# Weights split three blocks ahead of the products, with five blocks of high parts in place of four

## The chip, the cores and the metric

The kernel runs on one core of a Trainium2 chip. The metric is the device time of one execution in microseconds (us), the median of several. The engines are TensorE (PE; PEld is its weight load), VectorE (DVE), ScalarE (ACT), GpSimd (POOL) and SyncE (SP), which here only issues DMAs. Each runs its own list of instructions in order; they meet through semaphores.

## The reference

256 tokens behind 16 learned ones, width 1024, in fp32. First a hybrid block: one wide projection `w_in` feeds a gated delta rule (8 heads, chunks of 64), a sparse attention whose keys an indexer picks, and two gates; the two branches are mixed, and an MLP follows. Then a second block: a short convolution mixer, attention over a memory, a dense gated feed-forward, block attention, and a mixture of eight experts. The part around the change, in words of the reference:

```python
# delta branch
q, k, v = split(silu(causal_conv(cat(q, k, v), conv_w)))       # l2-normed, chunked delta rule
o = rmsnorm(o, norm_w) * silu(z)                                # "gated heads"
# sparse attention: score all keys with the indexer, keep the best, attend to them
s = einsum('bqhd,bsd->bqhs', qi, ki)
s = einsum('bqhs,bqh->bqs', relu(s), wi)
s = where(key_pos <= pos, s, -inf)
_, idx = lax.top_k(s, topk)                                     # topk = 64
p = softmax(where(valid, einsum(q, k_sel) * hd ** -0.5, -inf))
```

All matrix products with weights are meant at fp32 accuracy.

## The kernel before, in words

**Splitting.** TensorE multiplies in a rounded fp32 format (fp32r). For fp32 accuracy a factor is written as a high part (its rounding) and a low part (the rest), and a product is three matmuls, lines 433 to 435 in `mm3`: high by low, low by high, high by high.

**The stream of weights.** The weights are one long list `W` of blocks of up to 128 x 2048 numbers (1 MB), 143 before the experts and 33 for each expert. Four engines handle each block:
- SyncE loads it into a slot of the raw ring (line 396), 6 slots (8 in the experts), as soon as the block that held the slot is used;
- ScalarE casts it to its high part in a slot of the ring `hi_ring` (line 408). It waits for the block to land and, with NHI slots, for the products of block i - NHI;
- VectorE subtracts the high part from the raw block, in place (line 423), which leaves the low part;
- TensorE multiplies with both.

`act_high(q, upto)` casts all blocks up to number `upto` that aren't cast yet, at that place in ScalarE's list; `dve_low` does the same for VectorE. The calls are written into the code of each stage by hand, with the block whose products are next plus 2. Nothing else sets the order: each engine's list is fixed, and what it can't start yet holds what is behind it.

**Three low parts are GpSimd's.** `POOL_LOW` (line 411) names the blocks of aq 1 to aq 3, numbers 22 to 24; `dve_low` steps over them, and `pool_low` (line 429) makes them in stage index: two in a row, then the heads' gating (L1515, 8 instructions), then the third. av 0 is block 20, aq 0 block 21, gate_a 0 block 25.

**The stages** are load, delta, inverse, scan, index, dsa, mix, mlp, layer 0, dense, layer 1, experts. Two matter most here.

At the start TensorE multiplies the first blocks (the channels gk of the delta branch). ScalarE takes the results out of PSUM (L890, L897), VectorE runs the convolution's taps (L908), copies the 24 small columns out of PSUM (`dve_gate_small`, L766), and TensorE transposes these (L727).

In stage index TensorE multiplies the indexer's queries with its keys (L1608); ScalarE takes each head's scores through a relu out of PSUM (L1641), VectorE adds them up, weighed by head (L1682, `scalar_tensor_tensor` with two inputs in SBUF, 14 times). TensorE then sums the heads' squares (L1523) and goes on with the products of aq; ScalarE takes these out (L1632, `act_raw`). VectorE makes the norms (L1528, L1537) and then searches the best keys in `dve_best`: 8 rounds for each of two rows of queries, a MAX of eight (L1691) and a replacement (L1693), then the mask (L1697, L1699). Behind the search stand the gated heads (L1551), the ropes (L1575, L1581; L1565 on TensorE, L1570 on GpSimd), and the softmax rows of stage dsa.

Further places of the prediction: after `wo` (stage mix) the memory's keys and values (mk, mv) are multiplied, and VectorE copies them (L1982) ahead of the first blocks of the MLP.

Of the kernel before, what the change touches and what calls it, by code (L numbers as in the profile page):

```python
# [19 lines left out]
NRAW, NHI = 6, 4  # L20
# [243 lines left out]
def emit(A, cst, out, sem, counts, off, arena, arena_r, ring, ring_r, hi_ring, C, vec, sm, posi, ix, flag, bank):  # L264
# [799 lines left out]
    def act_delta_in(q):  # L1064
        for i in range(4):
            if i == 1:
                act_high(q, W.at["gk", 1] + 2)
                act_gate_rows(q)
            act_channels(q, "gk", i)
        act_silu(q, "gk", 7)  # L1070
        act_high(q, W.at["gq", 0] + 2)
# [24 lines left out]
        q.mark("delta_in")  # L1096

    def dve_delta_in(q):
        q.wait_ge(("in", "ident"))
        q.e.tensor_reduce(ident16, ident.rearrange("p (q c) -> p c q", c=16), AX, ALU.add).then_inc(*q.did(("ident16",)))  # L1100
        for i in range(4):
            if i == 1:
                dve_low(q, W.at["gk", 1] + 2)
# [173 lines left out]
    def act_base(q):  # L1277
        for r in range(4):
            act_high(q, W.at["gz", r] + 2)
            for j in (2 * r, 2 * r + 1):  # L1280
                q.wait_ge(("ps", "gz", j), ("ps", "vT", 16), ("ps", "l2", 15), ("metasq",), ("end", "delta_in", "pool"))
                q.e.activation(gz[:, j, :], B("gz", j)[:, 0:SEQ], ACT.Silu).then_inc(*q.did(("gz", j)))
                B.drop(("gz", j), ("gz", j))
                if j in (1, 4):
                    act_meta(q, {1: 2, 4: 4}[j])
                if j >= 6:
                    act_turn_blocks(q, groups[2 * j - 12])
                    act_turn_blocks(q, groups[2 * j - 11])
        act_meta(q, 8)

    def dve_base(q):
        dve_turn_blocks(q)
        for i in range(14, -1, -1):
            if i == 11:
                dve_meta_inverse(q, 1)
                dve_low(q, W.at["gz", 0] + 2)
            if i == 4:
                dve_low(q, W.at["gz", 1] + 2)
# [6 lines left out]
        dve_low(q, W.at["gz", 2] + 2)  # L1305
        dve_low(q, W.at["gz", 3] + 2)
# [142 lines left out]
    def act_scan(q):  # L1449
# [5 lines left out]
        for c in range(2):  # L1455
            for hp in range(0, 8, 4):
# [5 lines left out]
                act_high(q, W.at[name, r] + 2)  # L1462
# [7 lines left out]
    def dve_scan(q):  # L1470
# [4 lines left out]
        for c in range(2):  # L1475
            for hp in range(0, 8, 4):
                name, r, x0, n = BETWEEN[2 * c + hp // 4]
                dve_low(q, W.at[name, r] + 2)
# [165 lines left out]
    def act_index_in(q):  # L1644
        act_high(q, W.at["av", 0] + 2)
# [11 lines left out]
        for r in range(4):  # L1657
            act_high(q, W.at["aq", r] + 2)
# [42 lines left out]
    def dve_index_in(q):  # L1701
        dve_low(q, W.at["av", 0] + 2)
# [3 lines left out]
        dve_low(q, W.at["aq", 1] + 2)  # L1706
        dve_best(q)
        dve_low(q, W.at["aq", 2] + 2)
# [3 lines left out]
        dve_low(q, W.at["aq", 3] + 2)  # L1712
# [155 lines left out]
    def dve_branch_gates(q):  # L1868

        between = dve_ropes_between(q)  # L1870
        for name, dst in GATED:
            for r in range(4):
                for j in (2 * r, 2 * r + 1):
                    if j % 2:
                        dve_low(q, W.at[name, r] + 2)
# [6 lines left out]
    def act_branch_gates(q):  # L1882
        for name, dst in GATED:
            for r in range(4):
                act_high(q, W.at[name, r] + 2)
# [16 lines left out]
    def act_merge(q):  # L1902
        act_sigmoids(q)
        for r in range(4):
            act_high(q, W.at["wa", r] + 2)
        for r in range(4):
            act_high(q, W.at["wb", r] + 2)
# [6 lines left out]
    def dve_merge(q):  # L1914
        for r in range(4):
            dve_low(q, W.at["wa", r] + 2)
# [4 lines left out]
        for r in range(4):  # L1921
            dve_low(q, W.at["wb", r] + 2)
# [227 lines left out]
    def dve_mix(q):  # L2150
        for hf, k0, nk in row_blocks("wo", 8):
            dve_low(q, W.at["wo", hf, k0] + 2)
# [42 lines left out]
    def act_mlp(q):  # L2195
        for r in range(16):
            act_high(q, W.at["mlp_up", r] + 2)
# [11 lines left out]
        for hf, k0, nk in row_blocks("mlp_dn", 32):  # L2209
            act_high(q, W.at["mlp_dn", hf, k0] + 2)  # L2210
# [16 lines left out]
    def dve_mlp(q):  # L2227
        for r in range(16):
            dve_low(q, W.at["mlp_up", r] + 2)
# [6 lines left out]
        for hf, k0, nk in row_blocks("mlp_dn", 32):  # L2236
            dve_low(q, W.at["mlp_dn", hf, k0] + 2)
# [265 lines left out]
    def act_layer0(q):  # L2503
        for r in range(3):
            act_high(q, W.at["uc", r] + 2)
# [3 lines left out]
        for r in range(3):  # L2509
            act_high(q, W.at["uh", r] + 2)  # L2510
        act_high(q, W.at[("qm", 0), 0] + 2)
# [3 lines left out]
        for r in range(3):  # L2515
            act_high(q, W.at["ub", r] + 2)
# [3 lines left out]
        for hf, k0, nk in row_blocks(("o", 0), 8):  # L2520
            act_high(q, W.at[("o", 0), hf, k0] + 2)
# [4 lines left out]
    def dve_layer0(q):  # L2526
        for r in range(3):
            dve_low(q, W.at["uc", r] + 2)
# [3 lines left out]
        for r in range(3):  # L2532
            dve_low(q, W.at["uh", r] + 2)
# [9 lines left out]
        dve_low(q, W.at[("qm", 0), 0] + 2)  # L2543
        pairs = dve_pairs(q, mem0)
        for r in range(3):
            dve_low(q, W.at["ub", r] + 2)
# [8 lines left out]
        for hf, k0, nk in row_blocks(("o", 0), 8):  # L2555
            dve_low(q, W.at[("o", 0), hf, k0] + 2)
# [19 lines left out]
    def act_dense(q):  # L2576
        for j in range(11):
            act_high(q, W.at["dg", j] + 2)
# [8 lines left out]
            act_high(q, W.at["du", j] + 2)  # L2587
            for f in (2 * j, 2 * j + 1):
                act_split(q, gg.hi[:, f, :], gtmp[f % 4], ("gu", f), ("gghi", f))
        for hf, k0, nk in row_blocks("dd", 22):  # L2590
            act_high(q, W.at["dd", hf, k0] + 2)
# [4 lines left out]
    def dve_dense(q):  # L2596
        rest = dve_both_weighed(q, "a0")
        for j in range(11):
            dve_low(q, W.at["dg", j] + 2)
            dve_low(q, W.at["du", j] + 2)  # L2600
# [9 lines left out]
        for hf, k0, nk in row_blocks("dd", 22):  # L2610
            dve_low(q, W.at["dd", hf, k0] + 2)
# [40 lines left out]
    def act_layer1(q):  # L2652
        for r in range(3):
            act_high(q, W.at["kx", r] + 2)
# [3 lines left out]
        for r in range(3):  # L2658
            act_high(q, W.at["vx", r] + 2)
        for r in range(3):  # L2660
            act_high(q, W.at["qx", r] + 2)
# [4 lines left out]
        act_high(q, W.at[("qm", 1), 0] + 2)  # L2666
# [3 lines left out]
        for hf, k0, nk in row_blocks(("o", 1), 8):  # L2670
            act_high(q, W.at[("o", 1), hf, k0] + 2)
# [15 lines left out]
    def dve_layer1(q):  # L2687
        rest = dve_both_weighed(q, "b0")
        for r in range(3):
            dve_low(q, W.at["kx", r] + 2)  # L2690
# [5 lines left out]
        for r in range(3):  # L2696
            dve_low(q, W.at["vx", r] + 2)
# [5 lines left out]
        for r in range(3):  # L2703
            dve_low(q, W.at["qx", r] + 2)
# [4 lines left out]
        dve_low(q, W.at[("qm", 1), 0] + 2)  # L2709
# [4 lines left out]
        for hf, k0, nk in row_blocks(("o", 1), 8):  # L2714
            dve_low(q, W.at[("o", 1), hf, k0] + 2)
# [199 lines left out]
    def act_up(q, R, x):  # L2915
        for j, (c0, n, nk) in enumerate(UPS):
            act_high(q, R.w.at["up", x, j, 0, 8 - nk] + 2, R.w)
# [5 lines left out]
            act_high(q, R.w.at["up", x, j, 1, 8 - nk] + 2, R.w)  # L2923
# [378 lines left out]
```

## Time and profile before

| | |
|---|---|
| median of 3 runs | 1872.31 us (1871.34 to 1874.65) |
| the profiled execution | 1868.43 us, span 1866.6 us |
| mean granted clock of TensorE | 0.985 |
| TensorE busy | 1810.5 us, 97% |
| VectorE busy | 1393.0 us, 75% |
| ScalarE busy | 1073.5 us, 58% |
| GpSimd busy | 119.8 us, 6% |
| moved by DMA | 438.91 MB, mean 235 GB/s |

The span runs from the first to the last instruction of the profiled execution; busy times are shares of it. In rows of a timeline the first number is the start in us from the span's start, the second how long the group of `xN` like instructions took, and the bracket holds the idle time of the engine before it and what ended that. An arrow reads "written from". A clock of 1.00 is 2.4 GHz, 0.50 is 1.2 GHz.

### The profile page before, as it was taken

To read this page: it belongs to the slowest core of one execution; us is meant where nothing else is said; L and a number is where in the kernel's file an instruction comes from. 1 tells how busy PE (TensorE), PEld (TensorE's weight loads), DVE (VectorE), ACT (ScalarE), POOL (GpSimd) and SP (SyncE) were. 2 spreads that over 40 slices of the span, in tenths; PEclk is the share of its full clock that TensorE was granted. 3 is DMA by queue.
4 is the path that set the end of the run, shared out by engine and by line. 5 is a ranking of instruction groups with operands and counts; after the bars stand their busy time and mean duration, and the time that the engine had idled before them with its cause. 6 is when DMAs were issued, how large, how long until landed. Compare 5 with 4: busy or idle time off the path is not lost.

```text
span 1866.6 us, 26784 instructions
## 1 busy us (share of the span) xinstructions
PE 1810.5 (97%) x11434; PEld 1626.3 (87%) x11434; DVE 1393.0 (75%) x1621; ACT 1073.5 (58%) x1188; POOL 119.8 (6%) x123
## 2 busy tenths in 40 slices
PE   9999999999999999999998899999999999999997
PEld 8999988999998898998896788888888888888885
DVE  6796387566665466655675789898989898889887
ACT  7653344545554444543344477777767677777674
POOL 2353152000000000000010000000000000000000
PEclk9999989999999999999998799999999999999999
DMA  8332224455655454665553289989998999899993
GB/s 285 107 103 69 91 91 136 154 197 178 195 180 190 162 178 150 201 203 169 170 181 113 90 309 370 374 312 377 351 379 309 377 352 379 322 364 368 359 371 138
DMA packets 258983, 438.91 MB, mean 235 GB/s; under 512 B 10309, under 2 KB 131736, under 8 KB 258728
## 3 DMA queue, kind: packets, MB, share of 16 engines
q1 hardware_dynamic: 258856, 437.11, 67.1%
q8 instruction: 92, 1.51, 0.3%
q14 instruction: 35, 0.29, 0.0%
HBM read 436.04 MB, written 1.05 MB: 234 GB/s over the span
## 4 chain that ended last, share of the span: by engine, by line
PE 85%; DVE 5%; ACT 2%; issue 1%; POOL 0%; DVEq 0%; ACTq 0%; POOLq 0%
PE bank L435 25%; PE bank L433 25%; PE bank L434 25%; PE bank L2886 1%; PE bank L2833 1%; PE bank L1785 1%; DVE ring_r L423 1%; PE bank L2396 1%; PE bank L1331 1%; PE bank L1323 1%; ACT arena L2418 1%; DVE arena L1693 0%; DVE arena L1581 0%; PE bank L1336 0%; PE bank L2984 0%
## 5 line engine op out<-in xcount | busy, mean ns | idle before, releaser
L423 DVE TENSOR_TENSOR ring_r<-ring,hi_ring 128x2048 fp32r<-128x2048 f32 x403 | 910.3, 2286 | 261.8 <-ACT hi_ring L408 261.6
L408 ACT CAST hi_ring<-ring 128x2048 fp32r<-128x2048 f32 x406 | 761.4, 1904 | 151.7 <-PE bank L435 147.4
L433 PE MATMUL bank<-hi_ring,arena_r 128*128 128x512 f32 (+1 forms) x1542 | 573.9, 372 | 0.0
L434 PE MATMUL bank<-ring_r,arena_r 128*128 128x512 f32 (+2 forms) x1550 | 572.9, 370 | 0.0
L435 PE MATMUL bank<-hi_ring,arena_r 128*128 128x512 f32 (+1 forms) x1542 | 572.1, 371 | 0.0
L433 PE MATMUL bank<-ring_r,hi_ring 128*128 128x256 f32 (+1 forms) x1400 | 400.6, 286 | 6.0 <-DVE ring_r L423 2.7
L434 PE MATMUL bank<-ring_r,hi_ring 128*128 128x256 f32 (+1 forms) x1400 | 395.7, 283 | 0.0
L435 PE MATMUL bank<-ring_r 128*128 128x256 f32 (+1 forms) x1400 | 395.7, 283 | 0.0
L434 PEld LDWEIGHTS bank<-ring_r,arena_r 128*128 128x128 f32 (+1 forms) x1550 | 291.7, 188 | 51.6
L435 PEld LDWEIGHTS bank<-hi_ring,arena_r 128*128 128x128 f32 x1542 | 290.6, 188 | 50.5
L433 PEld LDWEIGHTS bank<-hi_ring,arena_r 128*128 128x128 f32 x1542 | 290.7, 188 | 50.2
L433 PEld LDWEIGHTS bank<-ring_r,hi_ring 128*128 128x128 f32 x1400 | 264.8, 189 | 8.6 <-DVE ring_r L492 3.1
L435 PEld LDWEIGHTS bank<-ring_r 128*128 128x128 f32 x1400 | 265.1, 189 | 0.0
L434 PEld LDWEIGHTS bank<-ring_r,hi_ring 128*128 128x128 f32 x1400 | 264.0, 189 | 0.2
L496 ACT CAST arena_r<-bank 128x512 fp32r<-128x512 f32 (+1 forms) x62 | 32.3, 526 | 73.3 <-PE bank L2886 66.6
L496 ACT CAST arena_r<-arena 128x256 fp32r<-128x256 f32 (+2 forms) x74 | 31.7, 432 | 72.5 <-DVE arena L2603 37.6
L2921 ACT ACTIVATE arena<-bank 128x512 f32<-128x512 f32 (+1 forms) x48 | 27.1, 564 | 68.2 <-PE bank L435 68.1
L492 DVE TENSOR_TENSOR arena_r<-bank,arena_r 128x512 fp32r<-128x512 f32 (+1 forms) x62 | 37.4, 607 | 12.5 <-ACT arena_r L496 12.5
L433 PE MATMUL bank<-arena_r,hi_ring 128*128 128x256 f32 x160 | 45.4, 284 | 0.0
L435 PE MATMUL bank<-arena_r,ring_r 128*128 128x256 f32 x160 | 45.3, 283 | 0.0
L434 PE MATMUL bank<-arena_r,hi_ring 128*128 128x256 f32 x160 | 44.9, 281 | 0.0
L1632 ACT ACTIVATE arena<-bank 128x256 f32<-128x256 f32 (+1 forms) x27 | 10.4, 385 | 57.0 <-PE bank L435 57.0
(397 smaller groups left out, 1621.9 us busy)
## 6 DMA issues: line engine op xcount, KB each, us to landing
ring<-in_w_gu_moe SPq DMA_DIRECT2D x176, 1024.0 KB, 6.2
ring<-in_w_down_moe SPq DMA_DIRECT2D x88, 1024.0 KB, 5.5
ring<-in_w_in SPq DMA_DIRECT2D x31, 1024.0 KB, 5.4
ring<-in_w_gu_dense SPq DMA_DIRECT2D x22, 1024.0 KB, 5.2
ring<-in_w_up SPq DMA_DIRECT2D x16, 1024.0 KB, 5.4
ring<-in_w_down SPq DMA_DIRECT2D x16, 1024.0 KB, 5.0
ring<-in_w_in_a SPq DMA_DIRECT2D x10, 1024.0 KB, 5.6
ring<-in_w_down_dense SPq DMA_DIRECT2D x10, 1024.0 KB, 5.1
```

The costliest lines, as they stand in the source:

```text
L408: q.e.copy(hi_ring[:, b:b + m], ring[:, a:a + m]).then_inc(*q.did(("hi", of.tag, i)))
L423: q.e.tensor_tensor(ring_r[:, a:a + m], ring[:, a:a + m], hi_ring[:, b:b + m].bitcast(F32), ALU.subtract).then_inc(*q.did(("lo", of.tag, i)))
L433: q.e.matmul(ps, a[0], b[0], start=first, stop=False)
L434: q.e.matmul(ps, a[0], b[1], start=False, stop=False)
L435: return q.e.matmul(ps, a[1], b[0], start=False, stop=last)
L492: q.e.tensor_tensor(lo, src, hi.bitcast(F32), ALU.subtract).then_inc(*q.did(*done))
L496: q.e.copy(hi, src).then_inc(*q.did(*done))
L1323: t = q.e.matmul(ps[:, x * P:(x + 1) * P], MTs[i % 3][:, x, :], D[:, m, :], start=True, stop=True)
L1331: t = q.e.matmul(ps[:, x * P:(x + 1) * P], Ys[i % 3][:, x, :], DT[:, m, :], start=True, stop=True)
L1785: t = q.e.matmul(ps[p0:p0 + hd, qt * P:(qt + 1) * P], u["v"](j)[0:n, :], pt[0:n, j, :], start=(x == 0), stop=(x == len(use) - 1))
L2396: t = q.e.matmul(ps[:, 65 * e:65 * e + 65], pt[:, x * P:(x + 1) * P], u["v"](j, 2 * e + par), start=(j == 0), stop=(j == nj - 1))
L2921: q.e.activation(hh[:, c0:c0 + n], R.banks(R.tag, "up", x, j, 0)[:, 0:n], ACT.Silu).then_inc(*q.did(("hsilu", R.tag, x, j)))
```

## The change

A constant AHEAD = 3 takes the place of the 2 at every call of `act_high` and `dve_low`; the ring of high parts gets a fifth slot (8 KB for each partition). The scratch memory that is set aside for dynamic DMAs is set to 4096 bytes when the program is built. The diff in its core (the same replacement stands at all other calls):

```diff
-NRAW, NHI = 6, 4
+NRAW, NHI, AHEAD = 6, 5, 3
...
     def act_channels(q, name, i):
         dst, w0, c0 = chan[name]
-        act_high(q, W.at[name, i] + 2)
+        act_high(q, W.at[name, i] + AHEAD)
...
     def dve_channels(q, name, i):
         dst, w0, c0 = chan[name]
-        dve_low(q, W.at[name, i] + 2)
+        dve_low(q, W.at[name, i] + AHEAD)
...
     def act_index_in(q):
-        act_high(q, W.at["av", 0] + 2)
+        act_high(q, W.at["av", 0] + AHEAD)
...
         for r in range(4):
-            act_high(q, W.at["aq", r] + 2)
+            act_high(q, W.at["aq", r] + AHEAD)
...
     def dve_index_in(q):
-        dve_low(q, W.at["av", 0] + 2)
+        dve_low(q, W.at["av", 0] + AHEAD)
...
-        dve_low(q, W.at["aq", 1] + 2)
+        dve_low(q, W.at["aq", 1] + AHEAD)
         dve_best(q)
-        dve_low(q, W.at["aq", 2] + 2)
+        dve_low(q, W.at["aq", 2] + AHEAD)
...
     def act_mix(q):
         for hf, k0, nk in row_blocks("wo", 8):
-            act_high(q, W.at["wo", hf, k0] + 2)
+            act_high(q, W.at["wo", hf, k0] + AHEAD)
...
     def dve_up(q, R, x):
         for j, (c0, n, nk) in enumerate(UPS):
-            dve_low(q, R.w.at["up", x, j, 0, 8 - nk] + 2, R.w)
-            dve_low(q, R.w.at["up", x, j, 1, 8 - nk] + 2, R.w)
+            dve_low(q, R.w.at["up", x, j, 0, 8 - nk] + AHEAD, R.w)
+            dve_low(q, R.w.at["up", x, j, 1, 8 - nk] + AHEAD, R.w)
...
-    nc = bacc.Bacc("TRN2", target_bir_lowering=False, num_devices=1)
+    nc = bacc.Bacc("TRN2", target_bir_lowering=False, num_devices=1, dynamic_dma_scratch_size=4096)
```

TensorE's list stays as it is. On VectorE, at the start of the program, before the first taps (L908); `ring_r` is the raw ring seen as fp32r, `hi_ring` the ring of high parts:

```order
 L423 TENSOR_TENSOR ring_r_49<-ring,hi_ring 128x2048
 L1100 TENSOR_REDUCE sm<-consts 128x16
-L423 TENSOR_TENSOR ring_r_49<-ring,hi_ring 128x2048
+L423 TENSOR_TENSOR ring_r_49<-ring,hi_ring 128x2048 x2
 L908 SCALAR_TENSOR_TENSOR arena<-bank2,vec,arena 128x271
 L908 SCALAR_TENSOR_TENSOR arena<-bank2,vec,arena 128x270
```

One subtraction more, that of block 3, stands ahead of the taps; ScalarE casts three blocks instead of two at that place.

On VectorE in stage index, between the norms of the heads and the search of the best keys:

```order
 L1684 TENSOR_TENSOR arena<-arena,consts 128x128
 L1537 RECIPROCAL sm<-sm 128x16
+L423 TENSOR_TENSOR ring_r_49<-ring,hi_ring 128x2048
 L1691 MAX arena<-arena 128x8
 L1693 MATCH_REPLACE arena<-arena 128x272
```

Before, nothing stood there, since block 24 is GpSimd's; now block 25 does.

On GpSimd in stage index, with the semaphores that each instruction waits for (act_index counts ScalarE's instructions of this stage):

```order
 L1510 TENSOR_TENSOR arena<-arena 128x256 x3
-L429 TENSOR_TENSOR ring_r<-ring,hi_ring 128x2048 [waits act_index] x2
-L1515 TENSOR_TENSOR arena<-arena 128x256 [waits act_inverse]
+L429 TENSOR_TENSOR ring_r<-ring,hi_ring 128x2048
+L429 TENSOR_TENSOR ring_r<-ring,hi_ring 128x2048 [waits act_index]
+L1515 TENSOR_TENSOR arena<-arena 128x256 [waits act_inverse,act_index]
 L1515 TENSOR_TENSOR arena<-arena 128x256 [waits act_inverse,pool_index]
```

The instructions are the same; what moved is what they wait for. The high part of block 22 is now cast in the stage before, and that of block 23 by the first instruction of ScalarE in this one.

## Rows read from the trace of the kernel before

**Rows 1.** Section 1 of the page: busy us, share of the span, instructions by engine

```profile
PE 1810.5 (97%) x11434; PEld 1626.3 (87%) x11434; DVE 1393.0 (75%) x1621; ACT 1073.5 (58%) x1188; POOL 119.8 (6%) x123
```

**Rows 2.** TensorE's waits: us in total, times, longest

```profile
PE bank L875 <- DVE sm L817: 2.9, 1, 2.9
PE bank L433 <- DVE ring_r L423: 2.7, 1, 2.7
...
PE bank L1608 <- ACT arena L1641: 2.2, 1, 2.2
...
PE bank L1785 <- ACT arena L1814: 2.0, 1, 2.0
```

**Rows 3.** Busy time by stretch: PE, PEld, DVE, ACT, POOL; then PEclk, DMA share, GB/s

```profile
200.00:250.00 50.00, 47.85 (x356) 45.18 (x355) 25.19 (x36) 20.15 (x39) 12.55 (x12) 0.92 0.32 99
250.00:300.00 50.00, 48.05 (x384) 46.57 (x381) 47.32 (x104) 23.25 (x40) 30.14 (x22) 0.98 0.41 127
300.00:448.00 148.00, 148.00 (x1126) 139.12 (x1124) 94.97 (x165) 77.12 (x138) 0.16 (x2) 1.00 0.51 168
1084.00:1866.00 782.00, 769.58 (x3701) 642.83 (x3699) 684.19 (x456) 554.02 (x409) 0.00 (x0) 1.00 0.95 345
```

**Rows 4.** Section 5 of the page, VectorE's subtraction for low parts

```profile
L423 DVE TENSOR_TENSOR ring_r<-ring,hi_ring 128x2048 fp32r<-128x2048 f32 x403 | 910.3, 2286 | 261.8 <-ACT hi_ring L408 261.6
```

**Rows 5.** Timeline of VectorE, 446 to 456 us: start, us, what, count, idle before

```profile
448.27 0.42 DVE L1982 COPY consts<-bank 128x256 f32<-128x256 f32 x1 [2.39 <-PE bank L435]
448.62 6.69 DVE L423 TENSOR_TENSOR ring_r<-ring,hi_ring 128x2048 fp32r<-128x2048 f32 x3
```

**Rows 6.** Section 3 of the page: queue, packets, MB, share

```profile
q1 hardware_dynamic: 258856, 437.11, 67.1%
```

**Rows 7.** Timeline of SyncE's queue, 0 to 30 us

```profile
13.26 5.30 SPq L396 DMA_DIRECT2D ring<-in_w_in  x3
```

**Rows 8.** Instructions of line 396 from 0 to 30 us, their landing

```profile
DMA to landing us min/median/max: 8.8/9.9/13.7
```

**Rows 9.** Timeline of VectorE, 23 to 28 us

```profile
23.68 3.04 DVE L908 SCALAR_TENSOR_TENSOR arena<-bank,vec,arena 128x271 f32<-128x271 f32 x6
...
26.69 0.40 DVE L766 COPY arena<-bank 24x272 f32<-24x272 f32 x1
```

**Rows 10.** Timeline of TensorE, 26 to 29 us

```profile
27.15 0.33 PE L727 MATMUL bank<-consts,arena 24*128 24x24 f32 x3
```

**Rows 11.** Timeline of ScalarE, 225 to 262 us

```profile
229.00 1.92 ACT L408 CAST hi_ring<-ring 128x2048 fp32r<-128x2048 f32 x1
...
240.23 0.29 ACT L1641 ACTIVATE arena<-bank 128x144 f32<-128x144 f32 x1 [0.18 <-DVE arena L1682]
...
257.25 1.90 ACT L408 CAST hi_ring<-ring 128x2048 fp32r<-128x2048 f32 x1
```

**Rows 12.** Timeline of VectorE, 230 to 300 us

```profile
252.93 0.38 DVE L1691 MAX8 arena<-arena 128x8 f32<-128x272 f32 x1
...
254.66 0.43 DVE L1691 MAX8 arena<-arena 128x8 f32<-128x272 f32 x1
...
272.45 2.71 DVE L1551 SCALAR_TENSOR_TENSOR arena<-arena,vec,bank 128x512 f32<-128x512 f32 x4
```

**Rows 13.** Instructions of line 1697: duration ns min/median/max

```profile
L1697 DVE TENSOR_SCALAR arena<-arena x2: 296/1320/2345, 267.1 to 269.7; 128x272 f32<-128x272 f32 x2
```

**Rows 14.** Timeline of GpSimd, 225 to 270 us

```profile
234.97 4.53 POOL L429 TENSOR_TENSOR ring_r<-ring,hi_ring 128x2048 fp32r<-128x2048 f32 x1
254.61 4.63 POOL L429 TENSOR_TENSOR ring_r<-ring,hi_ring 128x2048 fp32r<-128x2048 f32 x1 [15.11 <-ACT hi_ring L408]
...
264.78 4.53 POOL L429 TENSOR_TENSOR ring_r<-ring,hi_ring 128x2048 fp32r<-128x2048 f32 x1
```

**Rows 15.** Instructions of line 1682: duration ns min/median/max

```profile
L1682 DVE SCALAR_TENSOR_TENSOR arena<-arena,sm x14: 368/500/4456, 235.2 to 251.9; 128x144 f32<-128x144 f32 x7, 128x272 f32<-128x272 f32 x7
```

**Rows 16.** Timeline of TensorE, 236 to 246 us

```profile
240.75 5.47 PE L1523 MATMUL bank<-consts,arena 128*128 128x1 f32 x28
```

More of the change, by code:

```diff
@@ L1066, in act_delta_in @@
             if i == 1:
-                act_high(q, W.at["gk", 1] + 2)
+                act_high(q, W.at["gk", 1] + AHEAD)
                 act_gate_rows(q)
@@ L1070, in act_delta_in @@
         act_silu(q, "gk", 7)
-        act_high(q, W.at["gq", 0] + 2)
+        act_high(q, W.at["gq", 0] + AHEAD)
         act_gate_sums(q)
@@ L1102, in dve_delta_in @@
             if i == 1:
-                dve_low(q, W.at["gk", 1] + 2)
+                dve_low(q, W.at["gk", 1] + AHEAD)
                 dve_gate_rows(q)
@@ L1278, in act_base @@
         for r in range(4):
-            act_high(q, W.at["gz", r] + 2)
+            act_high(q, W.at["gz", r] + AHEAD)
             for j in (2 * r, 2 * r + 1):
@@ L1295, in dve_base @@
                 dve_meta_inverse(q, 1)
-                dve_low(q, W.at["gz", 0] + 2)
+                dve_low(q, W.at["gz", 0] + AHEAD)
             if i == 4:
-                dve_low(q, W.at["gz", 1] + 2)
+                dve_low(q, W.at["gz", 1] + AHEAD)
                 dve_meta_inverse(q, 2)
@@ L1304, in dve_base @@
         dve_meta_inverse(q, 4)
-        dve_low(q, W.at["gz", 2] + 2)
-        dve_low(q, W.at["gz", 3] + 2)
+        dve_low(q, W.at["gz", 2] + AHEAD)
+        dve_low(q, W.at["gz", 3] + AHEAD)
     steps = [(b, g) for b in (16, 32, 64) for g in groups[:4]]
@@ L1884, in act_branch_gates @@
             for r in range(4):
-                act_high(q, W.at[name, r] + 2)
+                act_high(q, W.at[name, r] + AHEAD)
                 yield
@@ L1904, in act_merge @@
         for r in range(4):
-            act_high(q, W.at["wa", r] + 2)
+            act_high(q, W.at["wa", r] + AHEAD)
         for r in range(4):
-            act_high(q, W.at["wb", r] + 2)
+            act_high(q, W.at["wb", r] + AHEAD)
             for j in (2 * r, 2 * r + 1):
@@ L1915, in dve_merge @@
         for r in range(4):
-            dve_low(q, W.at["wa", r] + 2)
+            dve_low(q, W.at["wa", r] + AHEAD)
             for j in (2 * r, 2 * r + 1):
@@ L1921, in dve_merge @@
         for r in range(4):
-            dve_low(q, W.at["wb", r] + 2)
+            dve_low(q, W.at["wb", r] + AHEAD)
             for j in (2 * r, 2 * r + 1):
@@ L2196, in act_mlp @@
         for r in range(16):
-            act_high(q, W.at["mlp_up", r] + 2)
+            act_high(q, W.at["mlp_up", r] + AHEAD)
             if r == 0:
@@ L2228, in dve_mlp @@
         for r in range(16):
-            dve_low(q, W.at["mlp_up", r] + 2)
+            dve_low(q, W.at["mlp_up", r] + AHEAD)
             for j in (2 * r, 2 * r + 1):
@@ L2504, in act_layer0 @@
         for r in range(3):
-            act_high(q, W.at["uc", r] + 2)
+            act_high(q, W.at["uc", r] + AHEAD)
             if r == 0:
@@ L2509, in act_layer0 @@
         for r in range(3):
-            act_high(q, W.at["uh", r] + 2)
-        act_high(q, W.at[("qm", 0), 0] + 2)
+            act_high(q, W.at["uh", r] + AHEAD)
+        act_high(q, W.at[("qm", 0), 0] + AHEAD)
         for j in range(2):
@@ L2515, in act_layer0 @@
         for r in range(3):
-            act_high(q, W.at["ub", r] + 2)
+            act_high(q, W.at["ub", r] + AHEAD)
             for j in (2 * r, 2 * r + 1):
@@ L2527, in dve_layer0 @@
         for r in range(3):
-            dve_low(q, W.at["uc", r] + 2)
+            dve_low(q, W.at["uc", r] + AHEAD)
             if r == 0:
@@ L2532, in dve_layer0 @@
         for r in range(3):
-            dve_low(q, W.at["uh", r] + 2)
+            dve_low(q, W.at["uh", r] + AHEAD)
             for j in (2 * r, 2 * r + 1):
@@ L2577, in act_dense @@
         for j in range(11):
-            act_high(q, W.at["dg", j] + 2)
+            act_high(q, W.at["dg", j] + AHEAD)
             if j == 0:
@@ L2598, in dve_dense @@
         for j in range(11):
-            dve_low(q, W.at["dg", j] + 2)
-            dve_low(q, W.at["du", j] + 2)
+            dve_low(q, W.at["dg", j] + AHEAD)
+            dve_low(q, W.at["du", j] + AHEAD)
             for f in (2 * j, 2 * j + 1):
@@ L2610, in dve_dense @@
         for hf, k0, nk in row_blocks("dd", 22):
-            dve_low(q, W.at["dd", hf, k0] + 2)
+            dve_low(q, W.at["dd", hf, k0] + AHEAD)
             if k0 == 20:
@@ L2653, in act_layer1 @@
         for r in range(3):
-            act_high(q, W.at["kx", r] + 2)
+            act_high(q, W.at["kx", r] + AHEAD)
             if r == 0:
@@ L2658, in act_layer1 @@
         for r in range(3):
-            act_high(q, W.at["vx", r] + 2)
+            act_high(q, W.at["vx", r] + AHEAD)
         for r in range(3):
-            act_high(q, W.at["qx", r] + 2)
+            act_high(q, W.at["qx", r] + AHEAD)
             if r == 0:
@@ L2665, in act_layer1 @@
                 act_scaled(q, "qx", j, qx)
-        act_high(q, W.at[("qm", 1), 0] + 2)
+        act_high(q, W.at[("qm", 1), 0] + AHEAD)
         for j in range(2):
@@ L2689, in dve_layer1 @@
         for r in range(3):
-            dve_low(q, W.at["kx", r] + 2)
+            dve_low(q, W.at["kx", r] + AHEAD)
             if r == 0:
@@ L2696, in dve_layer1 @@
         for r in range(3):
-            dve_low(q, W.at["vx", r] + 2)
+            dve_low(q, W.at["vx", r] + AHEAD)
             for c in range(2):
@@ L2703, in dve_layer1 @@
         for r in range(3):
-            dve_low(q, W.at["qx", r] + 2)
+            dve_low(q, W.at["qx", r] + AHEAD)
             if r:
@@ L2708, in dve_layer1 @@
                 next(rest)
-        dve_low(q, W.at[("qm", 1), 0] + 2)
+        dve_low(q, W.at[("qm", 1), 0] + AHEAD)
         next(rest)
```

38 lines of the change are left out of this document (19 added, 19 removed).

## The prediction

> **What bounds the kernel now.** I read the busy table first. TensorE is busy 97% of the span, VectorE 75%, ScalarE 58% [rows 1]. So a change to the casts can gain at most what TensorE stands idle, 1866.6 - 1810.5 = 56 us, and only what of that is a wait for a weight block. The list of TensorE's waits is the second view: of its waits only one is for the low part of a weight block, 2.7 us, once [rows 2]. The third view, busy time by stretch, shows the experts (from 1084 us, 42% of the span) with TensorE busy 769.58 of 782 us at clock 1.00, and the two stretches from 200 to 300 us with lower clocks, 0.92 and 0.98, and VectorE busy 47.32 of 50 us from 250 to 300 us [rows 3]. So cushion is plentiful where weights stream, and scarce where VectorE has its own long jobs. VectorE's low parts wait 261.6 us in all for ScalarE's casts, and cost nobody anything [rows 4]: in steady state they are throttled by the ring, since a cast may run only when TensorE has used the block whose slot it takes. That decides how the change reads.
>
> **The change part by part.** *Steady state.* A call site now asks for block p+3 instead of p+2, and the high ring has five slots instead of four, so the cast at that site waits for the same product as before (p+3-5 = p+2-4 = p-2). It runs when it ran, on a block one later: same count of casts and subtractions (403 of these on VectorE, 2286 ns each), one more block ready in advance. TensorE gets from it only waits for a block, of which there is one. That goes for mix, MLP, layer 0 and 1, dense and the experts: 0 us.
>
> *The wait at 450.95 us.* It ends 2.33 us after the start of a subtraction at 448.62, which stands behind a copy out of PSUM that waited for TensorE until 448.27 [rows 5]. The change puts four subtractions behind that copy instead of three; block 49 is still the first of them. The copy still gates it. Gain 0; the ceiling is 2.7.
>
> *wo to memory.* One cast (1.9) and one subtraction (2.3) move ahead of the row sums of the mix stage; TensorE has two blocks of products of its own then. 0, with at most 2.3 if that cover were gone.
>
> *Scratch.* All weight traffic is in one queue that SyncE issues, 437.11 MB [rows 6]; GpSimd issues no DMA. Its scratch is memory that pays for the fifth slot. 0.
>
> *The start.* Before the first channel evictions (L890) ScalarE now casts three blocks in a row, and VectorE subtracts two in a row before L908. The third of these, block 3, is in the group of three issued from 13.26; these DMAs land 8.8 us or more after issue, so it is there at about 22.1 [rows 7, 8]. Now: cast 22.1 to 24.0, subtraction 24.0 to 26.3, and L908, which began at 23.68, begins at about 26.3: 2.6 later. Behind it L766 (small columns out of PSUM, 26.69) ends at 29.7; TensorE's transposes of these, L727, began at 27.15 with no idle time before them [rows 9, 10]. TensorE waits 2.3 (the subtraction alone) to 2.6 us. Does it come back? From there to 74 us ScalarE, VectorE and TensorE pass the evictions, gates and norms to one another, and TensorE then waits 2.9 us for VectorE's L817 [rows 2]; all three are late by the same amount, so that wait stays. Taken: **+2.5**.
>
> *The index stage.* Here the numbering matters. Low parts of aq 1 to 3 (blocks 22 to 24) are GpSimd's; aq 1 + 2 = 24 was skipped by VectorE before the top-k search (dve_best), but aq 1 + 3 = 25 is gate_a 0, which isn't. So a subtraction of 2.29 us stands before L1691, and it waits for a cast that ScalarE makes only after both raw copies of aq 1, at 257.25 to 259.15 [rows 11]. The search began at 252.93 [rows 12]. It is 16 rounds, 14.2 us, and the searched rows, then L1551 (frees the banks of the gated heads), ropes, one more subtraction and softmax rows stand behind it on VectorE up to 296.38, where TensorE waits 2.0 for ScalarE L1814, whose data come from VectorE [rows 2]. VectorE has 47.32 of 50 us of work there, and TensorE is busy without a gap from 300 to 448 [rows 3], so nothing later takes a delay back. Gated thus: 259.15 - 252.93 = 6.2 of waiting, 2.29 of subtraction, less 2.05 because one of the two L1697 (2345 ns against 296 for the other) stood behind GpSimd's third L429, 264.78 to 269.31 [rows 13, 14], and will run when that is done. **+6.4** if nothing else moves.
>
> Something else moves. At its first site in the stage ScalarE (229.00) now casts block 23, not 22. GpSimd's second L429, which waited 15.1 us for ScalarE until 254.61, will follow the first at once: 239.5 to 244.0 [rows 14]. What the first did is in the rows: beside it (234.97 to 239.50) one L1682, two inputs in SBUF, took 4456 ns where the shortest takes 368 and the median 500, and TensorE waited 2.2 us for ScalarE's L1641 behind it [rows 2, 15]. A second L429 right behind would hold the next L1682 to 244.2 instead of 240.18; ScalarE's next L1641 goes from 240.23 to 244.2, and TensorE's L1523, which began at 240.75, to about 244.5: 3.7 later [rows 11, 16]. Then aq 1 ends 3.7 later, the cast of 25 is done at 262.85, the subtraction at 265.1, the search begins at 265.1 instead of 252.93: 12.2, less the same 2.05: **+10.1**. TensorE would show it as about 3.7 at L1523, and the rest where it needs the banks that L1551 frees (272.45, now 282.6 [rows 12]) and at 296.
>
> A rule bears on which of the two it is. The Trainium skill, "SBUF — State Buffer", section "Who interferes with whom", says that a VectorE instruction with two SBUF inputs, or one in a two-port mode (a tensor_scalar can be), shares a pair of ports with GpSimd, that who issues first keeps it for the whole instruction, and that other VectorE instructions aren't held. The trace agrees: 4456 ns for L1682 and 2345 for L1697 beside an L429, and 0.43 us for L1691 at 254.66, beside the second L429 [rows 12 to 15]. By the rule the term is +10.1 if GpSimd gets the pair at 239.5 and +6.4 to +8 if VectorE does.
>
> The clock: the idle 2.2 us at 240 was followed by clock 0.92 for the stretch 200 to 250 [rows 3], 50 x 0.08 = 4 us of full-speed work lost. A longer idle there may lengthen it, where TensorE's own work is hidden behind VectorE's to 296. Bounds 0 and +4; taken +0.5.
>
> **Sum.** Own time of the profiled execution 1868.4 + 2.5 + 10.1 + 0.5 = 1881.5. That execution lies 3.9 below the median of the runs, 1872.3; the same sum on the median is 1885.4. I forecast **1885.4 us**.
>
> **The rivals.**
> A. VectorE isn't held a second time (it slips in between, or the data of block 23 are late so that GpSimd starts later): +2.5 + 6.4 = +8.9, 1881.2. For it: at 239.5 both engines have the next instruction ready, so that who comes first is a matter of tenths; against it: GpSimd's second then waits for nothing, and VectorE's first L1682 still runs.
> B. The search is not the bound: TensorE's waits in the stage are short (2.2 and 2.0), perhaps the chain has slack that I don't see, so that only the start is paid: 1874.8, within what can be told from no change (0.2%, 3.7 us). Against it: VectorE is busy 47.32 of 50 us there.
> C. Not slower. The longer lead decides everything where a low part was late: the wait at 450.95 goes (-2.7), and the 2.05 us of L1697 comes off the path because the subtraction before the search finds its cast ready. That needs the cast of block 25 done before 252.8, the point from which it decides; ScalarE would then have to cast it ahead of the raw copies of aq 1, and its order forbids this. Price: -2.7 - 2.05 = -4.8, 1867.6; with the start's +2.5 kept 1870.1, no change.
> D. More than forecast: +10.1 and the clock drops again at each new wait, near 245 and near 280, and the 2.3 of wo to memory shows: 10.1 + 2.5 + 4 + 2.3 = +19, to 1891.
> E. The change doesn't do what it says where it could: casts at steady sites run when they ran, and the two odd sites hide behind TensorE. 1872.3.
>
> **How the numbers follow.** Forecast 0.45; A 0.28; D 0.08; B 0.08; E 0.04; C 0.07 (0.05 of it at 1867.6, the rest at 1870). Slower by over 0.2%: 0.45 + 0.28 + 0.08 = 0.81. Same: B, E and part of C, 0.14. Faster 0.05. The range holds forecast, A and D and what the execution-to-median step of 3.9 may be off: 1876 to 1892.
>
> **What would show it.** In the profile after: L1691 begins at about 261 (A) or 265 (forecast), with an idle time before VectorE's L423 that ScalarE's L408 ended; two L1682 of over 4 us instead of one; TensorE waiting near 27 for L766 for 2.5 us, near 240 to 244 for L1641 some 6 us in place of 2.2, and before 284 for L1551; the wait at 450.95 still 2.7; experts as long as before, 782 us for the same work. Wrong would be: L1691 at 253 (the order or the numbering was misread), experts shorter by more than 2 us (then the lead was worth something in steady state), or TensorE's total idle time grown by less than 5 us.

## The result, and the profile after

The changed kernel takes 1884.78 us (median of 5 runs, 1883.53 to 1886.43), the one before 1872.31 (1868.89 to 1877.20, 5 runs): ratio 1.0065, 95% interval 1.005 to 1.008. It is slower by 12.5 us. The forecast was 1885.4. The profiled execution took 1883.53 us, its span is 1881.7, 15.1 more than the one before. One execution behind this document, of search_gate_alone, took 6816.1 us where its other five took 1882.3 to 1888.1; it is left out of times and ratios, and why it took so long isn't known.

VectorE, ScalarE and GpSimd are busy as before; the time went into TensorE, in part as idle time and in part as a lower clock. Section 1 of its page, which answers to [rows 1]:

```profile
PE 1817.6 (97%) x11434; PEld 1631.5 (87%) x11434; DVE 1396.1 (74%) x1621; ACT 1074.7 (57%) x1188; POOL 117.6 (6%) x123
```

With the same 11434 matmuls TensorE is busy 7.1 us longer, and it idles 8.0 us longer (64.1 against 56.1). The list of its waits (us in total, times, longest) answers to [rows 2]:

```profile
PE bank L1565 <- DVE arena L1551: 4.7, 1, 4.7
...
PE bank L1523 <- ACT arena L1641: 3.3, 1, 3.3
...
PE bank L727 <- DVE arena L766: 3.1, 1, 3.1
PE bank L875 <- DVE sm L817: 2.9, 1, 2.9
PE bank L433 <- DVE ring_r L423: 2.7, 1, 2.7
...
PE bank L1608 <- ACT arena L1641: 2.1, 1, 2.1
...
PE bank L1785 <- ACT arena L1814: 0.7, 1, 0.7
```

Three lines are new: L727 (3.1 us) at the start, L1523 (3.3) and L1565 (4.7) in stage index. L875, L1608 and the 2.7 us behind L423 are as they were; the wait before L1785 has shrunk from 2.0 to 0.7. By stretch, to be read against [rows 3] (busy PE, PEld, DVE, ACT, POOL, then PEclk):

```profile
200.00:250.00 50.00, 44.60 (x351) 42.44 (x349) 25.90 (x31) 17.57 (x31) 19.50 (x17) 0.93 0.34 106
250.00:300.00 50.00, 45.28 (x307) 42.84 (x307) 37.43 (x87) 21.38 (x33) 15.46 (x16) 0.83 0.28 85
```

The clock stands at 0.93 and 0.83, where it was 0.92 and 0.98: over these 100 us, 12 us of full-speed work are lost against 5. Slices of 2 us show where: the granted clock was 0.50 from 244 to 260 us, where the waits at L1608 and L1523 lie, and from 288 to 294, where the wait at L1565 ends; before, it was 0.50 from 242 to 250, behind the one wait at L1608.

*The start*, [rows 9] and [rows 10]; VectorE's timeline (start, us, what), then ScalarE's, then TensorE's:

```profile
24.41 2.29 DVE L423 TENSOR_TENSOR ring_r<-ring,hi_ring 128x2048 fp32r<-128x2048 f32 x1 [0.80 <-ACT hi_ring L408]
26.62 3.04 DVE L908 SCALAR_TENSOR_TENSOR arena<-bank,vec,arena 128x271 f32<-128x271 f32 x6
...
29.64 0.40 DVE L766 COPY arena<-bank 24x272 f32<-24x272 f32 x1
```

```profile
22.47 1.92 ACT L408 CAST hi_ring<-ring 128x2048 fp32r<-128x2048 f32 x1 [1.85 <-DMA ring<-in_w_in]
```

```profile
30.09 0.33 PE L727 MATMUL bank<-consts,arena 24*128 24x24 f32 x3 [3.08 <-DVE arena L766]
```

The third cast waited 1.85 us for its block to land, the second subtraction follows, and L908, L766 and L727 are all 2.9 us later.

*Stage index.* GpSimd's timeline, ScalarE's, VectorE's and TensorE's, to be read against [rows 14], [rows 11], [rows 12] and [rows 16]:

```profile
238.51 9.05 POOL L429 TENSOR_TENSOR ring_r<-ring,hi_ring 128x2048 fp32r<-128x2048 f32 x2
...
262.69 4.62 POOL L429 TENSOR_TENSOR ring_r<-ring,hi_ring 128x2048 fp32r<-128x2048 f32 x1 [9.14 <-ACT hi_ring L408]
```

```profile
265.49 1.90 ACT L408 CAST hi_ring<-ring 128x2048 fp32r<-128x2048 f32 x1
```

```profile
238.75 12.73 DVE L1682 SCALAR_TENSOR_TENSOR arena<-arena,sm 128x144 f32<-128x144 f32 x7
...
260.84 0.25 DVE L1537 RECIPROCAL sm<-sm 128x16 f32<-128x16 f32 x1
267.42 2.29 DVE L423 TENSOR_TENSOR ring_r<-ring,hi_ring 128x2048 fp32r<-128x2048 f32 x1 [6.32 <-ACT hi_ring L408]
269.63 0.44 DVE L1691 MAX8 arena<-arena 128x8 f32<-128x272 f32 x1
...
287.70 2.72 DVE L1551 SCALAR_TENSOR_TENSOR arena<-arena,vec,bank 128x512 f32<-128x512 f32 x4
```

```profile
248.16 2.08 PE L1523 MATMUL bank<-consts,arena 128*128 128x1 f32 x9 [3.25 <-ACT arena L1641]
```

```profile
288.50 2.08 PE L1565 MATMUL bank<-arena,consts 128*128 128x256 f32 x4 [4.72 <-DVE arena L1551]
```

The two L429 are one row now, 9.05 us without a gap, and the seven L1682 beside them take 12.73 us (7.30 before). The subtraction before the search waited 6.32 us for ScalarE's cast of block 25, the one at 265.49; L1691 begins at 269.63, against 252.93. Line 1682 as a whole (duration ns min/median/max), and line 1697, to [rows 15] and [rows 13]:

```profile
L1682 DVE SCALAR_TENSOR_TENSOR arena<-arena,sm x14: 500/644/4459, 238.7 to 259.9; 128x144 f32<-128x144 f32 x7, 128x272 f32<-128x272 f32 x7
```

```profile
L1697 DVE TENSOR_SCALAR arena<-arena x2: 288/358/429, 283.9 to 285.0; 128x272 f32<-128x272 f32 x2
```

TensorE's L1785 begins at 311.43, where it began at 296.38: 15.05 later. The 2.7 us wait for block 49 ends at 466.01 instead of 450.95, 15.06 later, and the span ends 15.1 later. After 311 us nothing was gained or lost.

### The profile page after: what moved, and what is told of

Read it like the earlier page. It is cut to its first block, busy times and chain, and to the rows that moved or that the text cites. A ratio compares the mean times of both kernels' runs of the same rounds, so it can differ in the third digit from the quotient of the medians.

```text
span 1881.7 us, 26780 instructions
## 1 busy us (share of the span) xinstructions
PE 1817.6 (97%) x11434; PEld 1631.5 (87%) x11434; DVE 1396.1 (74%) x1621; ACT 1074.7 (57%) x1188; POOL 117.6 (6%) x123
## 4 chain that ended last, share of the span: by engine, by line
PE 85%; DVE 5%; ACT 2%; issue 1%; POOL 0%; DVEq 0%; ACTq 0%; POOLq 0%
PE bank L435 25%; PE bank L434 25%; PE bank L433 25%; PE bank L2886 1%; PE bank L2833 1%; PE bank L1785 1%; DVE ring_r L423 1%; PE bank L2396 1%; PE bank L1331 1%; PE bank L1323 1%; ACT arena L2418 1%; PE bank L1565 0%; DVE arena L1682 0%; DVE arena L1693 0%; ACT hi_ring L408 0%
## 5 line engine op out<-in xcount | busy, mean ns | idle before, releaser
L423 DVE TENSOR_TENSOR ring_r<-ring,hi_ring 128x2048 fp32r<-128x2048 f32 x403 | 910.1, 2285 | 265.3 <-ACT hi_ring L408 265.1
L408 ACT CAST hi_ring<-ring 128x2048 fp32r<-128x2048 f32 x406 | 761.5, 1904 | 155.2 <-PE bank L435 128.8
L492 DVE TENSOR_TENSOR arena_r<-bank,arena_r 128x512 fp32r<-128x512 f32 (+1 forms) x62 | 37.4, 608 | 12.5 <-ACT arena_r L496 12.5
```

Of the source, the lines that this page charges most:

```text
L408: q.e.copy(hi_ring[:, b:b + m], ring[:, a:a + m]).then_inc(*q.did(("hi", of.tag, i)))
L423: q.e.tensor_tensor(ring_r[:, a:a + m], ring[:, a:a + m], hi_ring[:, b:b + m].bitcast(F32), ALU.subtract).then_inc(*q.did(("lo", of.tag, i)))
L492: q.e.tensor_tensor(lo, src, hi.bitcast(F32), ALU.subtract).then_inc(*q.did(*done))
```

## Experiments

Each was compared with runs of the kernel before on the same chip; the ratio is to these, with its 95% interval. "Own" is its profiled execution. The kernel before had a median of 1869.95 us beside the first four experiments, 1871.15 beside only_ring, pool_early, mlp_early and both_early, and 1871.65 beside the other two. So compare the ratios between experiments, not the medians.

### Putting back one place at a time

**VectorE's lead out of stage index.**

```diff
 def dve_index_in(q):
...
-        dve_low(q, W.at["aq", 1] + AHEAD)
+        dve_low(q, W.at["aq", 1] + 2)
         dve_best(q)
-        dve_low(q, W.at["aq", 2] + AHEAD)
+        dve_low(q, W.at["aq", 2] + 2)
...
-        dve_low(q, W.at["aq", 3] + AHEAD)
+        dve_low(q, W.at["aq", 3] + 2)
...
-                        dve_low(q, W.at[name, r] + AHEAD)
+                        dve_low(q, W.at[name, r] + (2 if name == "gate_a" else AHEAD))
```

> The changed kernel, but VectorE's three calls in stage index and those of gate_a ask for +2 as before, so that no subtraction stands before the search. ScalarE and GpSimd are as changed. My theory: the second L429 still holds L1682 (two of over 4 us, TensorE's 3.3 us at L1523 stays), but the search begins right behind L1537, near 261 instead of 269.6, and L1551 near 278.6 instead of 287.7: 8.9 us less than the changed kernel, its profiled execution at about 1874.6 against 1883.5. Rival (the search is not the bound, TensorE is): only the 4.7 us wait before L1565 goes, 1878.8. Rival (the ring or the scratch costs the time): no change, 1883.5.

Measured: 1880.21 us, ratio 1.0048 (1.0030 to 1.0066), own 1883.64. VectorE's timeline:

```profile
239.25 12.72 DVE L1682 SCALAR_TENSOR_TENSOR arena<-arena,sm 128x144 f32<-128x144 f32 x7
...
261.52 0.39 DVE L1691 MAX8 arena<-arena 128x8 f32<-128x272 f32 x1
...
278.99 2.71 DVE L1551 SCALAR_TENSOR_TENSOR arena<-arena,vec,bank 128x512 f32<-128x512 f32 x4
```

L1691 at 261.52 and L1551 at 278.99 are where my theory had them (its program began 0.5 us later), the two held L1682 stay (12.72 us), and the wait before L1565 is gone. But L1785 came at 304.88, 25.9 us after L1551, not 24: only 7.0 us were gained by there. TensorE was busy for all of the 50 us from 250 to 300, at a clock of 0.90: its own work had become the bound, so the rival is partly right once the gate is gone. 1.2 more were lost behind gate_b, where the lead was taken up again: two subtractions in a row made TensorE wait 0.95 us for L1830 at 333.

The expected 1874.6 us for its own execution was missed by far: it took 1883.64, no less than the changed kernel. Of the gain, 5.3 us are still there at 460.70, where the wait for block 49 ends (466.01 in the changed kernel), and 3.8 at 645.88. These go between 1000 and 1084 us, with no new wait of TensorE but a clock of 0.77 in place of 0.83. That is one execution. By the ratio 0.17% of 0.65% came back (3 us of 12), less than I expected, and part of that shortfall isn't explained.

**ScalarE's lead out of the first call of stage index.**

```diff
 def act_index_in(q):
-        act_high(q, W.at["av", 0] + AHEAD)
+        act_high(q, W.at["av", 0] + 2)
```

> The changed kernel, but ScalarE's first call of stage index asks for +2, so it casts nothing there and block 23 is cast near 256, when the head scores are done. All else as changed, the subtraction before the search too. My theory: one L1682 of over 4 us instead of two, no wait at L1523 (3.3 us), the cast of block 25 near 260.8, the search at about 265 instead of 269.6: 4.6 us less, profiled execution about 1878.9. Rival (VectorE slows beside GpSimd for another reason than what GpSimd runs at that moment): L1682 still 4.4 us twice, 1883.5.

Measured: 1879.71 us, ratio 1.0037 (1.0020 to 1.0053), own 1881.43. GpSimd's and VectorE's timelines:

```profile
239.39 4.54 POOL L429 TENSOR_TENSOR ring_r<-ring,hi_ring 128x2048 fp32r<-128x2048 f32 x1
260.25 4.64 POOL L429 TENSOR_TENSOR ring_r<-ring,hi_ring 128x2048 fp32r<-128x2048 f32 x1 [16.32 <-ACT hi_ring L408]
```

```profile
239.63 7.29 DVE L1682 SCALAR_TENSOR_TENSOR arena<-arena,sm 128x144 f32<-128x144 f32 x7
...
264.95 2.77 DVE L423 TENSOR_TENSOR ring_r<-ring,hi_ring 128x2048 fp32r<-128x2048 f32 x1 [6.29 <-ACT hi_ring L408]
```

One L429 beside the scores, one held L1682 (7.29 us for the seven), no wait at L1523. That step stands. The search began 2.0 us earlier than in the changed kernel, 2.9 with the start of its program taken out, not 4.6: TensorE reached the products 3.4 earlier, and the subtraction itself now met GpSimd's L1515 and took 2.77 instead of 2.29.

**The lead out of delta and inverse** (`+ 2` at the 10 calls of these stages, both engines).

> The changed kernel, with +2 as before in the stages delta and inverse on both engines; the lead of 3 begins in stage scan. My theory: TensorE's wait of 3.1 us at L727 and the low clock behind it (0.5 us) go and nothing else changes: 3.6 us less, about 1879.9. Rival (the delay at 30 us would be made up later anyway): the wait goes, but the index stage begins when it did, 1883.5.

Measured: 1881.17 us, ratio 1.0053 (1.0038 to 1.0067), own 1881.6. The wait at L727 is gone; L1224 begins 2.6 us before that of the changed kernel, the search 2.3, and the wait for block 49 ends at 462.54, 3.5 before. So the rival is out: what is lost at 30 us isn't made up by the index stage. Of the 3.5 its own time shows 1.9: between that point and L2042 near 648 it took 1.5 us longer than the changed kernel, with the same waits and a clock of 0.81 and 0.84 in the two slices of 5 us from 460 to 470.

**All three**, with ScalarE's other calls in stage index and gate_a at + 2 too.

> The changed kernel with +2 in delta, inverse, index and gate_a on both engines; five slots, 4096 bytes of scratch and the lead of 3 in scan, gate_b and all from merge on stay. My theory: the three places were all of the cost, 1868.4 as before, ratio 1.000. Rival (ring, scratch or the lead in the streaming stages costs something too): some us above. Rival (the lead is worth something there, hidden so far): below 1868.

Measured: 1873.54 us, ratio 0.9999 (0.9982 to 1.0015), own 1874.54. With the lead of 3 left in all other stages, the kernel is as fast as before. So the cost is in these places, and the lead is worth nothing elsewhere that could be told from noise (0.16%). One small cost is left in the trace: TensorE waits 0.95 us for L1830 at 328, where the lead is taken up again. The median is 3.6 us above that of the kernel before beside it, the mean 0.5: the times of both kernels are spread over 8 us and more, so that the median alone says little. The three single gains (0.17, 0.28, 0.12%) make 0.57 of 0.65%; they overlap in stage index. None of the three is clear of the intervals (the changed kernel's is 1.005 to 1.008), so what each place costs rests on the traces; the times show their sum.

### One suspect alone, on the kernel before

**Five slots and 4096 bytes, no lead** (`NRAW, NHI, AHEAD = 6, 5, 2`).

> Five slots of high parts and 4096 bytes of scratch, all calls at +2: the changed kernel without its lead. My theory: nothing of the cost is in the memory; the profiled execution at 1868.4 as before, but for the pieces of low clock that differ from one execution to the next (each takes 1.7 us), ratio 1.000. Rival (the fifth slot moves the ring onto memory that costs something, or the scratch does): ratio 1.002 or more.

Measured: 1872.94 us, ratio 1.0010 (0.9997 to 1.0024), own 1869.45. No cost that can be told from none. The two experiments below are this kernel with one call changed.

**Two L429 beside the head scores.**

```diff
-        act_high(q, W.at["av", 0] + AHEAD)
+        act_high(q, W.at["av", 0] + 3)
```

> only_ring, and ScalarE's first call of stage index alone asks for +3, so that GpSimd makes the low parts of 22 and 23 in a row beside the head scores, as in the changed kernel. No subtraction stands before the search. My theory: two L1682 of over 4 us, TensorE waits some 3.5 us at L1523, the search begins 4 to 4.7 us later than before, and 2.05 come back at L1697: 2.5 to 3 us more, about 1871. Rival (VectorE is held by GpSimd only now and then): one L1682 over 4 us, 1868.4.

Measured: 1877.53 us, ratio 1.0026 (1.0011 to 1.0041), own 1873.50. TensorE's waits and VectorE's timeline:

```profile
PE bank L1523 <- ACT arena L1641: 3.8, 1, 3.8
```

```profile
235.46 12.72 DVE L1682 SCALAR_TENSOR_TENSOR arena<-arena,sm 128x144 f32<-128x144 f32 x7
...
257.72 0.39 DVE L1691 MAX8 arena<-arena 128x8 f32<-128x272 f32 x1
```

12.72 us for seven L1682 and 3.8 us at L1523 from this one edit; against only_ring the search began 4.2 later and L1785 came 4.2 later, 3.3 with the shift of 0.9 that stood at L1224 taken out. The expected 2.5 to 3 were a little low.

**A subtraction before the search.**

```diff
-        dve_low(q, W.at["aq", 1] + AHEAD)
+        dve_low(q, W.at["aq", 1] + 3)
```

> only_ring, and VectorE's call before the search alone asks for +3, so that the subtraction of block 25 stands before the search instead of behind it. My theory: it waits 6.2 us for ScalarE's cast of 257.25 to 259.15, the search begins near 261.4, one subtraction fewer stands behind it and L1697 isn't held: L1551 4.2 us later than before, 1872.6. Rival (the search is not on the path): L1551 as late as that, but TensorE without a new wait there, 1868.4.

Measured: 1884.23 us, ratio 1.0066 (1.0042 to 1.0090), own 1884.97. VectorE's and GpSimd's timelines, and TensorE's wait:

```profile
267.34 6.05 DVE L423 TENSOR_TENSOR ring_r<-ring,hi_ring 128x2048 fp32r<-128x2048 f32 x1 [12.37 <-ACT hi_ring L408]
273.31 0.43 DVE L1691 MAX8 arena<-arena 128x8 f32<-128x272 f32 x1
...
288.62 2.72 DVE L1551 SCALAR_TENSOR_TENSOR arena<-arena,vec,bank 128x512 f32<-128x512 f32 x4
```

```profile
266.71 4.54 POOL L429 TENSOR_TENSOR ring_r<-ring,hi_ring 128x2048 fp32r<-128x2048 f32 x1
```

```profile
PE bank L1565 <- DVE arena L1551: 11.4, 1, 11.4
```

My number was wrong by a step: with ScalarE at +2, block 25 is not cast behind the raw copies of aq 0 (that cast is block 24's) but behind those of aq 1, at 265.41. So the subtraction waited 12.4 us, and then, with two inputs in SBUF, stood 3.8 us behind GpSimd's third L429 (6.05 us in all). The delay is twice the one I meant to set, and that makes the test a stronger one: the search began 19.8 us later than in only_ring and L1551 15.6 (1.5 of both stood there at L1224 already), TensorE waited 11.4 at L1565, L1785 came 14.1 later, and the ratio went from 1.0010 to 1.0066, some 10 us. The rival, that the search isn't on the path, is out.

### A better place for two low parts

These rest on only_ring. **GpSimd's first low part earlier:**

```diff
-                act_high(q, W.at[name, r] + AHEAD)
+                act_high(q, W.at[name, r] + AHEAD + {("iq", 1): 1, ("ik", 0): 2}.get((name, r), 0))
...
 def pool_scan(q):
...
-        pool_rope(q, ("ik",), ik, cc("cosI"))
+        pool_low(q, POOL_LOW[0]); pool_rope(q, ("ik",), ik, cc("cosI"))
...
 def pool_index_in(q):
         pool_heads_squared(q)
-        for i in POOL_LOW[0:2]:
+        for i in POOL_LOW[1:3]:
             pool_low(q, i)
         pool_heads(q)
-        pool_low(q, POOL_LOW[2])
```

> only_ring, and GpSimd makes the low part of block 22 before the ropes of stage scan (ScalarE casts it near 215), those of 23 and 24 behind the head scores. My theory (an L429 beside L1682 costs what it takes): no L1682 over 1 us, TensorE's wait of 2.2 at L1608 goes, the low clock behind it too, the search begins about 4 us earlier, and L1697 isn't held (2.05): 4 to 6 us less where TensorE isn't the bound, ratio 0.997 to 0.998. Rival (TensorE's own work from 236 to 296 becomes the bound): 2.2 to 4 us less.

Measured: 1864.25 us, ratio 0.9966 (0.9951 to 0.9981), own 1864.19: faster than both kernels. GpSimd's and VectorE's timelines:

```profile
216.79 4.88 POOL L429 TENSOR_TENSOR ring_r<-ring,hi_ring 128x2048 fp32r<-128x2048 f32 x1 [33.58 <-ACT hi_ring L408]
...
250.95 9.22 POOL L429 TENSOR_TENSOR ring_r<-ring,hi_ring 128x2048 fp32r<-128x2048 f32 x2 [15.36 <-ACT hi_ring L408]
```

```profile
235.78 3.20 DVE L1682 SCALAR_TENSOR_TENSOR arena<-arena,sm 128x144 f32<-128x144 f32 x7
...
249.27 0.39 DVE L1691 MAX8 arena<-arena 128x8 f32<-128x272 f32 x1
```

No L429 runs between 222 and 251; the seven L1682 take 3.20 us in place of 7.30, TensorE has no wait at L1608, and the search begins at 249.27. L1785 comes at 292.52 against 296.38. The 6.3 us of the ratio are a little more than the 4 to 6 that I expected. Of the 2.05 of L1697 only 0.7 came back, since GpSimd's L1515 now runs beside the mask. And the low clock didn't go with the wait:

```profile
200.00:250.00 50.00, 50.00 (x386) 47.34 (x385) 24.14 (x45) 23.47 (x44) 12.93 (x12) 0.93 0.33 103
```

TensorE is busy for all of the 50 us and still the clock reads 0.93, where it was 0.92 with the wait. The slices show it fall near 241 us, in the row of 32 matmuls of one column each (L1523), and stay low until 247. So the wait of 2.2 us isn't needed for it. What makes the clock fall stays open; in the changed kernel it fell near 243 us, in the wait at L1608 and before L1523.

**Block 49 ahead of the copy of mv 1:**

```diff
-        act_high(q, W.at[("mv", 1), 0])
+        act_high(q, W.at[("mv", 1), 0] + 1)
...
-        dve_memory(q, 1)
+        dve_low(q, W.at[("mv", 1), 0] + 1); dve_memory(q, 1)
```

> only_ring, and the first block of the MLP (49) is cast behind that of mv 1 and its low part made before VectorE copies mv 1, a wait of VectorE of 2.4 us. My theory of the wait at 450.95 (the copy gates it, not the lead): it goes, 2.7 us less than only_ring, ratio to before 0.9985. Rival (another wait is behind it, for the norm's columns or a bank): less than 1 us.

Measured: 1871.52 us, ratio 0.9999 (0.9987 to 1.0011), own 1871.67. **Both:**

> mlp_early and pool_early together, on five slots and +2. My theory: the gains add, 2.7 + 4 to 6 = 7 to 9 us less than before, ratio about 0.996. Rival: they overlap, as after a wait that goes the next is as long: 5 or less, 0.9975.

Measured: 1866.15 us, ratio 0.9967 (0.9951 to 0.9983), own 1864.93. The wait is gone from both lists, so the copy and not the lead set it; but the 2.7 us that I expected of it are in neither median. In the profile of both_early the clock took it back. Busy time by stretch (PEclk is the third number from the end), of pool_early and then of both_early:

```profile
625.00:760.00 135.00, 128.34 (x1005) 122.36 (x1005) 89.46 (x133) 60.91 (x78) 0.11 (x1) 1.00 0.52 172
```

```profile
625.00:760.00 135.00, 128.34 (x980) 122.35 (x980) 87.19 (x129) 60.32 (x76) 0.11 (x1) 0.97 0.53 171
```

0.03 of 135 us is 4 us of full-speed work. That is one execution each, and that the removed wait brought the low clock on isn't shown: dve_index_2, start_2 and all_sites_2 kept the wait and have such a dip right behind it, between 455 and 470 us. The fastest executions point the other way: 1866.27 in mlp_early against 1868.69 before, 1860.60 in both_early against 1862.90 in pool_early, 2.4 and 2.3 us less. Whether the wait is worth its 2.7 us stays open.

## Why the prediction was right

- *Steady state, scratch, fifth slot: 0.* Held: from 311 us to the end the two kernels stand 15.05 to 15.15 us apart, and only_ring shows 1.0010 with 1 in the interval.
- *The wait at 450.95: 0.* Held; it is 2.7 us at 466.01, behind four subtractions that begin at 463.67. Its removal by another edit shows what gates it.
- *wo to memory: 0.* Held, same distance before and behind.
- *The start: +2.5.* Right in place and kind, a little small. The block landed late enough to make it 2.9, and TensorE's wait was 3.1. At L1224 in stage inverse the kernels were 3.6 apart: the clock from 0 to 50 us was 0.97 with that wait in it, against 1.00. start_2 gives back 2.6 at L1224 and 3.5 at block 49.
- *The gate of the search.* Held: idle time 6.32 us before VectorE's L423, ended by ScalarE's L408 (6.2 said), and 1.9 of the 2.05 of L1697 came back (429 ns at most, from 2345). One name is wrong: the cast at 257.25, and the one at 265.49 that now gates, stand behind the raw copies of aq 0 and ahead of those of aq 1. The place is right, and the sum doesn't change; in search_gate_alone the name mattered.
- *The second L429.* Held: two L1682 are held, L1523 comes 3.8 us later with the start's shift taken out (3.7 said). Alone it is worth 0.16% over only_ring, with intervals that overlap; its trace shows 3.3 us.
- *Index in all: +10.1 and 0.5 of clock* against 11.5 (15.05 less 3.6). The part that was short is mainly the clock, which I put down at its lower end. On the path to the search, all of L1523 now ran at 0.50, 6.99 us instead of 6.32, and the search began 13.1 us later with the start's shift taken out, not 12.2. What the low clock was put down to, the idle time at 240, isn't needed for it: in pool_early that wait is gone and the clock falls all the same. In all 12 against 5 us of full-speed work were lost, and most of the rest was hidden behind VectorE: by L1785 the index stage had cost 11.5. There it showed at L1523 and L1565 alone, not at L1785, where I had put a part of it.
- *The sum* 13.1 against 15.1 between profiled executions, 12.5 between medians. Each term had the right place and sign; the median's forecast, 1885.4, is only 0.6 off, in part by luck: the profiled execution of before lay 3.9 below its median, that of after only 1.3.

The Trainium skill ("SBUF — State Buffer", "Who interferes with whom") says that the engine which issues first keeps the shared ports for the whole instruction, and leaves open who comes first at the seam of the two L429. The trace shows it: GpSimd's two took 4.54 and 4.57 us without a gap. The first L1682 ended at 243.21, just behind the end of the first L429 (ScalarE's L1641 waited 4.27 us for it, until 243.30), and the next was held again (4.23, until 247.82). The hold also shows for the subtraction, which has two SBUF inputs: 6.05 us beside an L429 and 2.77 beside L1515, against 2.29.

Rivals: A (no second hold) fell with the L1682 rows; its condition, that VectorE slips in between, came true for one L1682 and saved nothing, as the next met the second L429. The +8 that the prediction gives for this side has no working. B, C and E (search not the bound, not slower, all hidden) fell with search_gate_alone and with L1785. D's clock drops came, near 244 and 288, but not its 19 us.

## What to carry to other kernels

A lead that is written as "block number + n" moves work at every call where the list is irregular: at the start of a stream, where blocks of another engine are stepped over, and ahead of long jobs. Look at those calls one by one; where the stream was regular, the longer lead changed nothing here (ratio 0.9999). Work given to an idle engine isn't free if that engine then holds up the one it relieves: here the place of GpSimd's 4.5 us subtractions, the first of them above all, was worth 0.34% of the whole kernel.

## What was not expected of the hardware

- Executions of one and the same kernel spread over 8 us (only_ring: 1869.5 to 1877.4, twelve of them), and where two traces with the same waits over a stretch differed there, it was in the granted clock: all_sites_2 fell another 1.6 us behind the kernel before between L1608 and L1785, with a clock of 0.94 from 250 to 300 us and not 0.98. An effect of 0.2% needs its place in the trace, not medians alone.
- A wait of TensorE that was taken away (2.7 us) gave nothing in the medians; the profile of both_early shows a lower clock at a later stretch instead, and the fastest executions are 2.3 and 2.4 us faster.
- GpSimd's L1515 (eight instructions) took 7.66 us beside the subtraction in act_av_2 and 5.63 beside the search in the kernel before: the hold works both ways.
